# Final norm of a mixture-of-experts layer: nine token tiles beside the last two experts

## The reference, cut to what matters

```python
def rmsnorm(x, g):
    xf = x.astype(jnp.float32)
    y = xf * lax.rsqrt(jnp.mean(xf * xf, axis=-1, keepdims=True) + EPS)
    return (y * g.astype(jnp.float32)).astype(x.dtype)

def ec_moe(h, w_router, w_g, w_u, w_d):
    cap = EC_FACTOR * n // N_EXPERTS
    aff = jax.nn.softmax((h @ w_router).astype(jnp.float32), axis=-1)
    vals, idx = lax.top_k(aff.transpose(0, 2, 1), cap)
    xg = jax.vmap(lambda hb, ib: hb[ib])(h, idx)
    ...
    y = jnp.einsum('becf,efd->becd', jax.nn.silu(a) * u, w_d) * vals[..., None].astype(h.dtype)
    return ...zeros((n, D)).at[ib.reshape(-1)].add(yb.reshape(-1, D))

    x = x + g2 * ec_moe(h2, ...)
    y_prompt, y_sample = rmsnorm(xp, final_norm), rmsnorm(xs, final_norm)
```

## Time and profile before

| | |
|---|---|
| runs shown (3) | 3118.61, 3133.28, 3135.63 us |
| median | 3133.28 us |
| profiled execution | span 3119.0 us from first to last instruction; no time of its own is given beside the span |
| mean granted TensorE clock | 0.965 |
| instructions | 43740 |

### The profile page before, as it was taken

How to read it: one execution, slowest core, us unless ns; L and a number is a source line. 1 busy time by engine, 2 the same in 40 slices (tenths; PEclk the granted TensorE clock), 3 DMA queues, 4 the chain that set the end, 5 groups by cost and what they waited for, 6 DMA issues and landing times. The chain is left out here.

```text
span 3119.0 us, 43740 instructions
## 1 busy us (share of the span) xinstructions
PE 2902.1 (93%) x16786; PEld 2329.5 (75%) x16786; DVE 1992.4 (64%) x2606; ACT 1086.4 (35%) x1720; POOL 1066.2 (34%) x688
## 2 busy tenths in 40 slices
PE   6999999999789999999999999989937999999993
PEld 3888888888667777777777767878826888888882
DVE  5418292829348888878888865555675556566655
ACT  5311111111344444444444443223313333433344
POOL 1000000000123344444333546421106765656652
PEclk8999999999889999999999999999968999999996
DMA  6212232211541110110111146675414666666657
GB/s 231 100 51 106 80 105 80 106 66 55 185 139 24 27 32 13 27 34 16 23 27 33 34 132 191 190 251 165 154 59 156 200 203 200 188 202 206 202 184 285
DMA packets 139523, 371.24 MB, mean 119 GB/s; under 512 B 20886, under 2 KB 47996, under 8 KB 129116
## 3 DMA queue, kind: packets, MB, share of 16 engines
q1 hardware_dynamic: 99820, 266.47, 25.8%
q0 software_dynamic: 23984, 74.71, 8.7%
q10 hardware_dynamic: 15552, 27.79, 2.5%
HBM read 265.99 MB, written 102.89 MB: 118 GB/s over the span
## 5 line engine op out<-in xcount | busy, mean ns | idle before, releaser
L1176 ACT ACTIVATE at_w<-banks 128x512 f32<-128x512 f32 (+1 forms) x592 | 347.6, 591 | 467.1 <-PE banks L1282 410.9
L1398 DVE TENSOR_REDUCE at_mpart<-banks 128x2 f32<-128x512 f32 x584 | 374.1, 683 | 140.2 <-PE banks L1309 140.0
L1254 POOL TENSOR_TENSOR at_part<-at_part,at_w 128x512 f32<-128x512 f32 x224 | 296.8, 1325 | 331.1 <-ACT at_w L1176 327.8
L2598 POOL TENSOR_TENSOR moe_gu_lo<-raw,moe_gu_hi 128x2048 fp32r<-128x2048 f32 x63 | 293.3, 4660 | 110.7 <-ACT moe_gu_hi L2665 110.3
L517 DVE SCALAR_TENSOR_TENSOR fr_r<-fr_r,fr_dw 128x2334 f32<-128x2334 f32 x120 | 318.0, 2650 | 3.9
L374 PE MATMUL fr_po<-hT_hi,fr_w_hi 128*128 128x512 f32 (+1 forms) x800 | 297.0, 371 | 3.0 <-PE fr_po L374 1.8
L374 PE MATMUL fr_po<-hT_lo,fr_w_hi 128*128 128x512 f32 (+1 forms) x800 | 294.7, 368 | 0.0
L374 PE MATMUL fr_po<-hT_hi,fr_w_lo 128*128 128x512 f32 (+1 forms) x800 | 294.7, 368 | 0.0
L1321 PE MATMUL banks<-at_w,V 128*64 128x256 f32 (+1 forms) x2368 | 283.0, 381 | 0.0
L2786 DVE TENSOR_TENSOR moe_d_lo<-moe_raw_d,moe_d_hi 128x1024 fp32r<-128x1024 f32 x64 | 198.1, 3095 | 106.4 <-ACT moe_d_hi L2697 106.4
L1425 DVE TENSOR_TENSOR at_part<-at_part,at_w 128x512 f32<-128x512 f32 x224 | 231.7, 1034 | 13.0
(11 more groups left out here) (415 smaller groups left out, 6805.9 us busy)
## 6 DMA issues: line engine op xcount, KB each, us to landing
raw<-w_gate_up SPq DMA_DIRECT2D x64, 1024.0 KB
moe_raw_d<-w_down SPq DMA_DIRECT2D x64, 512.0 KB, 4.5
fr_wm<-w_ada_rows POOLq DMA_DIRECT2D x32, 512.0 KB, 4.5
gates_scratch<-fr_r ACTq DMA_DIRECT2D x64, 256.0 KB, 2.0
mx_gates<-gates_scratch SPq DMA_DIRECT2D x64, 256.0 KB, 3.1
fr_raw<-w_in SPq DMA_DIRECT2D x28, 512.0 KB, 5.4
fr_r<-x POOLq DMA_DIRECT2D x18, 512.0 KB, 5.6
raw<-mixed_scratch SPq DMA_DIRECT2D x9, 1024.0 KB, 6.2
```

What stands on the lines that cost most here:

```text
L1176: act.activation(w[:, g % NW, k, 0:n], sc[:, (2 * g + k) % SCB, 0:n], ACT.Exp, scale=SM_SCALE).then_inc(exp_done, 1)
L1254: pool.tensor_tensor(part[:, j % 2, 1, 0:n], before, w[:, g % NW, 1, 0:n], ALU.add).then_inc(add_p, 1)
L1398: dve.tensor_reduce(mpart[:, s, 2 * half:2 * half + 2, c], max_bank(m, half), AX.X, ALU.max).then_inc(red_done, 1)
L2598: pool.tensor_tensor(gu_lo[:, slot], raw_gu[:, slot], gu_hi[:, slot].bitcast(F32), ALU.subtract).then_inc(glo_done, 1)
```

## The change

Tiles 0 to 8 are loaded during the last expert: SP issues the norm's weights and tiles 0 to 2 behind the down weights of piece 60 (after waiting for the scatter of expert 13), tiles 3 to 5 behind those of piece 61, tiles 6 to 8 behind those of piece 62; tiles 9 to 17 come as before, after the scatter of expert 14. Tiles 0 to 7 are normed in pairs at the ends of pieces 59, 60, 61 and 62 and stored by POOL one piece later. Tiles 8 to 11 are done in the last piece, at the place where 0 to 3 were. Behind it come three groups of three (12 to 14, 15 to 17, and 18 to 20). Within a group all squares are done first, then all roots, all reciprocals, all scalings.

Numbers 18 to 20 are new: since tiles 0 to 8 are now read before expert 14 adds its part, that expert's rows (two times 128 and 32 of full width) are gathered again after its scatter into weight buffers that are free by then (`old_rows`), normed like tiles, and written over the tiles' rows; only then are the rows of expert 15 written. The scatter of expert 14 now waits for the loads of tiles 0 to 8. Six semaphores are new, and two earlier phases clear a few of theirs at their end (`p.numbers`).

```diff
@@ attention_phase and mix_phase @@
+        p.numbers.append(norm_ld.num)
+        p.numbers += [sem.num for sem in (*c_ld, *o_st, inv_ld)]
@@ moe_phase @@
-    BEFORE, LATE, LATER = 4, 9, 13
+    DONE_IN = {(E - 2, 3): (0, 1), (E - 1, 0): (2, 3), (E - 1, 1): (4, 5), (E - 1, 2): (6, 7), (E - 1, 3): (8, 9, 10, 11)}
+    AFTER = ((12, 13, 14), (15, 16, 17), (18, 19, 20))
+    LOAD_IN = ((0, 1, 2), (3, 4, 5), (6, 7, 8), range(9, TILES))
...
+        old_rows = [raw[:, 0:D], raw[:, D:2 * D], raw_d[0:CAPP, 0]]
+        old_ld, old_st = p.sems("old_ld", 3), p.sems("old_st", 3)
+        def rows_of(n):
+            return fx[:, n % U] if n < TILES else old_rows[n - TILES]
...
@@ SP, in load(), behind the down weights @@
+                        if last:
+                            load_tokens(m)
+                def load_tokens(m):
+                    if m == 0:
+                        load_norm()
+                    if m in (0, M - 1):
+                        for i in range(3):
+                            sp.wait_ge(y_st[i], 16 * (E - 2 if m == 0 else E - 1))
+                    for n in LOAD_IN[m]:
+                        if n >= U:
+                            sp.wait_ge(f_st[n % U], 16 * (n // U))
+                        j = ORDER[n]
+                        sp.dma_start(fx[:, n % U], t["x2"][j * P:(j + 1) * P, :]).then_inc(fx_ld[n % U], 16)
@@ POOL, scatter() @@
+                    if isinstance(e, int) and e == E - 2:
+                        for n in range(U):
+                            pool.wait_ge(fx_ld[n], 16)
@@ POOL, gather_rows(), behind the gathers of expert 15's rows @@
+                    pool.wait_ge(glo_done, M * E - 1)
+                    pool.wait_ge(d_mm, M * E - 3)
+                    for i, (_, n) in enumerate(SL):
+                        pool.indirect_dma_start(old_rows[i], None, t["x2"],
+                                                bass.IndirectOffsetOnAxis(ap=idx_s[0:n, 0, i:i + 1], axis=0)).then_inc(old_ld[i], 16)
+                def store_tokens(ns):
+                    for n in ns:
+                        pool.wait_ge(f_done, n + 1)
+                        j = ORDER[n]
+                        pool.dma_start(t["y"][j * P:(j + 1) * P, :], fx[:, n % U]).then_inc(f_st[n % U], 16)
@@ POOL, expert() and behind it @@
+                        if last and m < M - 1:
+                            store_tokens(done_in(*((e, m - 1) if m else (e - 1, M - 1))))
                         if m == 2 and last:
                             gather_rows()
+                            store_tokens(done_in(e, m))
...
-                pool.wait_ge(out_done, 3)
+                store_tokens(range(8, TILES))
                 for u in range(U):
                     pool.wait_ge(f_st[u], 16 * (TILES // U))
+                pool.wait_ge(f_done, TILES + 3)
+                pool.sem_inc(may_issue, 1)
+                for i, (_, n) in enumerate(SL):
+                    pool.indirect_dma_start(t["y"], bass.IndirectOffsetOnAxis(ap=idx_s[0:n, 0, i:i + 1], axis=0), old_rows[i], None
+                                            ).then_inc(old_st[i], 16)
+                for i in range(3):
+                    pool.wait_ge(old_st[i], 16)
+                pool.wait_ge(out_done, 3)
@@ ACT; DVE has normed(ns) in the same places @@
-                            for n in range(BEFORE):
-                                squares(n)
+                            squares(done_in(e, m))
...
+                        if not (last and m == M - 1):
+                            squares(done_in(e, m))
                 pairs(act, expert)
-                for n in range(BEFORE, LATE):
-                    squares(n)
+                for ns in AFTER:
+                    squares(ns)
                 for i in range(2):
                     act.wait_ge(z_done, i + 1)
...
-                for n in range(LATE, LATER):
-                    squares(n)
                 act.wait_ge(zms_done, 2)
                 act.activation(root_l[:], mean_l[:], ACT.Sqrt).then_inc(zroot_done, 1)
-                for n in range(LATER, TILES):
-                    squares(n)
@@ DVE, normed(ns) @@
+                    for n in ns:
+                        u, c = n % U, rows_of(n).shape[0]
+                        dve.wait_ge(sq_done, n + 1)
+                        wait(dve, root_done, n - U + 1)
+                        dve.tensor_scalar(meansq[0:c, u:u + 1], sumsq[0:c, u:u + 1], 1.0 / D, EPS, ALU.mult, ALU.add).then_inc(ms_done, 1)
+                    for n in ns:
+                        u, c = n % U, rows_of(n).shape[0]
+                        dve.wait_ge(root_done, n + 1)
+                        dve.reciprocal(rstd[0:c, u:u + 1], root[0:c, u:u + 1]).then_inc(rstd_done, 1)
...
+                    for n in ns:
+                        u, x = n % U, rows_of(n)
+                        c = x.shape[0]
+                        dve.wait_ge(rstd_done, n + 1)
+                        dve.scalar_tensor_tensor(out=x, in0=x, scalar=rstd[0:c, u:u + 1], in1=norm[0:c],
+                                                 op0=ALU.mult, op1=ALU.mult).then_inc(f_done, 1)
```

More of the change, by code:

```diff
@@ L2512, in moe_phase, with done_in @@
             p.sem("norm_ld"), p.sems("fx_ld", U), p.sems("f_st", U), p.sems("row_ld", 3), p.sems("row_st", 3))
+        old_ld, old_st = p.sems("old_ld", 3), p.sems("old_st", 3)
+        def rows_of(n):
+            return fx[:, n % U] if n < TILES else old_rows[n - TILES]
+        def done_in(e, m):
+            return DONE_IN.get((e, m), ()) if isinstance(e, int) else ()
         sq_done, ms_done, root_done, rstd_done, f_done = (
@@ L2671, in x_hi_part, with squares @@
                                    turned_in(e, i, half)[:, 0:4 * n].rearrange("p (k n) -> p k n", k=4), ACT.Copy).then_inc(xhi_done, 1)
-                def squares(n):
-                    u = n % U
-                    act.wait_ge(fx_ld[u], 16 * (n // U) + 16)
-                    wait(act, sq_done, n - 1)
-                    wait(act, rstd_done, n - U + 1)
-                    act.activation(fsq[:, n % 2], fx[:, u], ACT.Square, accum_out=sumsq[:, u:u + 1]).then_inc(sq_done, 1)
-                    act.wait_ge(ms_done, n + 1)
-                    act.activation(root[:, u:u + 1], meansq[:, u:u + 1], ACT.Sqrt).then_inc(root_done, 1)
+                def squares(ns):
+                    for n in ns:
+                        u, x = n % U, rows_of(n)
+                        c = x.shape[0]
+                        if n < TILES:
+                            act.wait_ge(fx_ld[u], 16 * (n // U) + 16)
+                        else:
+                            act.wait_ge(old_ld[n - TILES], 16)
+                        wait(act, sq_done, n - 1)
+                        wait(act, rstd_done, n - U + 1)
+                        act.activation(fsq[0:c, n % 2], x, ACT.Square, accum_out=sumsq[0:c, u:u + 1]).then_inc(sq_done, 1)
+                    for n in ns:
+                        u, c = n % U, rows_of(n).shape[0]
+                        act.wait_ge(ms_done, n + 1)
+                        act.activation(root[0:c, u:u + 1], meansq[0:c, u:u + 1], ACT.Sqrt).then_inc(root_done, 1)
                 split_gu(0, 0, 0)
@@ L2757, in scale_y, with normed @@
                                              op0=ALU.mult, op1=ALU.mult).then_inc(y_done, 1)
-                def normed(n):
-                    u = n % U
-                    dve.wait_ge(sq_done, n + 1)
-                    wait(dve, root_done, n - U + 1)
-                    dve.tensor_scalar(meansq[:, u:u + 1], sumsq[:, u:u + 1], 1.0 / D, EPS, ALU.mult, ALU.add).then_inc(ms_done, 1)
-                    dve.wait_ge(root_done, n + 1)
-                    dve.reciprocal(rstd[:, u:u + 1], root[:, u:u + 1]).then_inc(rstd_done, 1)
-                    dve.wait_ge(rstd_done, n + 1)
-                    dve.scalar_tensor_tensor(out=fx[:, u], in0=fx[:, u], scalar=rstd[:, u:u + 1], in1=norm[:],
-                                             op0=ALU.mult, op1=ALU.mult).then_inc(f_done, 1)
+                def normed(ns):
+                    for n in ns:
[3 more added lines that the diff above has]
+                        dve.tensor_scalar(meansq[0:c, u:u + 1], sumsq[0:c, u:u + 1], 1.0 / D, EPS, ALU.mult, ALU.add).then_inc(ms_done, 1)
+                    for n in ns:
+                        u, c = n % U, rows_of(n).shape[0]
+                        dve.wait_ge(root_done, n + 1)
+                        dve.reciprocal(rstd[0:c, u:u + 1], root[0:c, u:u + 1]).then_inc(rstd_done, 1)
+                    if ns == DONE_IN[E - 2, M - 1]:
+                        dve.wait_ge(norm_ld, 16 * 6)
+                    for n in ns:
+                        u, x = n % U, rows_of(n)
+                        c = x.shape[0]
+                        dve.wait_ge(rstd_done, n + 1)
+                        dve.scalar_tensor_tensor(out=x, in0=x, scalar=rstd[0:c, u:u + 1], in1=norm[0:c],
+                                                 op0=ALU.mult, op1=ALU.mult).then_inc(f_done, 1)
```

(10 more changed lines are left out.)

20 lines of the change are left out of this document (6 added, 14 removed).

## The result

Before takes 3131.03 us (median of 20 runs, 3118.61 to 3135.88), the change 3135.65 us (20 runs, 3129.48 to 3141.33). The ratio is 1.0018 [1.0011, 1.0025]: slower by 0.18%, some 5.6 us. That is within the 0.5% named beforehand and inside the range, but the interval is clear of 1, and the sum had said -0.6 us.

A forecast was written before the change was run, and what follows sets the result against it. PE was taken to bound the experts up to 3051, then ACT, DVE and POOL the last 68 us. A loss of 13.5 us less a gain of 14.1 gave -0.6 us, 3132.7 us on the median; range 3115 to 3144.

The forecast's parts named there:

- The loop that is not hidden: Pieces 59 to 63: norm work stands in the loop ACT, DVE, POOL and loses 13.5 us before the tail.
- The wait of 3.7 us forecast before piece 63: End of piece 61: PE, ready at 3055.1, waits 3.7 us for gu_lo(63), then is 7.7 us late.
- The collision: DVE's tile scaling and POOL's subtraction hold each other; bounds: none, or up to 1.2 us on POOL, 4.6 on DVE per piece.
- The tail: From the end of d_hi(63) to POOL's final stores: 40.1 us instead of 54.2, a gain of 14.1 us.
- the ring comes round late: Rival, tail: loads wait for stores of earlier tiles; +2 us by medians, up to +6.4 (3139); chance 0.12.
- point of decision: Ring rival, tile 17's load behind tile 8's store: decides once a store and a load together take over 11.6 us.
- The argument against the rival: Against a late ring in the tail: traffic is now spread, nine loads are over before it.
- Groups save about 3: Tail check: grouping tiles saves about 3 us; a group of three costs 4.5 us against 5.4.
- The end: Final stores to kernel end: 12.5 us as before, from 3105.9 to 3118.4.
- Table switches: Rival: six added switches (nine for three) each hold ACT for twice the load, sum grows 7.7 us to 3140; chance 0.03.
- Hidden after all: Rival, last expert: d_hi(63) late only by its own pair, 3.9 us; total -10.2 us, 3123; chance 0.12.
- The level: Whole kernel: the runs' median is 14.3 us above the profiled execution; the difference is put on the median, giving 3132.7 us.

The follow-up runs named there:

- noin: The change with tiles 0 to 8 still loaded early but none normed in pieces 59 to 62 (0 to 3 in piece 63): 3135.93 us, ratio 1.0020.
- spare: The change with tiles 15, 16 and 17 loaded into free weight buffers, so their loads wait for no store: 3132.21 us, ratio 0.9999.
- late: The change with the gathers of expert 14's rows issued behind the stores of tiles 8 to 11: 3129.55 us, ratio 0.9994.
- sparelate: The change with tiles 15 to 17 in free weight buffers and expert 14's gathers behind the stores of tiles 8 to 11: 3132.11 us, ratio 1.0000.
- group: The kernel before with its tiles in groups, all squares of a group first, then roots, reciprocals, scalings: 3133.8 us, ratio 1.0013.
- best2: The change with twelve buffers, one pair at piece 59, tiles 2 to 5 singly in piece 63, old rows gathered behind tile 5's store: 3129.32 us, ratio 0.9998.
- copyroot: The change with the Sqrt of the tiles replaced by a Copy, which needs no table load: 3134.04 us, ratio 1.0008.
- best3: As best2, but expert 14's rows gathered where the change has them, ahead of the stores: 3130.09 us, ratio 1.0004.
- alt12: As noin12, but tiles 0 and 1 normed at the end of piece 59, 2 and 3 at the end of 61: 3131.66 us, ratio 0.9994.
- best: As best2, but expert 14's rows gathered behind the store of tile 11: 3131.82 us, ratio 1.0004.
- noin12: As noin, with a ring of twelve buffers in place of nine: 3132.1 us, ratio 0.9988.

## Why the prediction was right or wrong

**The sign of the sum was wrong; the size is 5.5 us off.** By its own terms, each taken from the x_hi copy:

- *The loop that is not hidden, +13.5.* Measured +11.34: right in mechanism, 2.2 too much. The piece at 61 fits to a few tenths (gu_hi forecast to end at 3026.5, measured 3026.3 after the shift of 7.13), and `noin` shows that nothing else costs here. What was too much is no single step: ACT's copies end 0.2, 0.7, 1.5 and 2.2 us ahead of the forecast from pair to pair (gu_hi of 61, 62 and 63, then d_hi). POOL's subtraction starts beside DVE's scaling and is stretched by 0.5 to 0.65, and so ends only 0.1 to 0.2 us before a full wait for the scaling would let it; the rest is steps that I rounded up. gu_lo(62) starts at 3039.1 where I put 3040.6, gu_lo(63) at 3051.9 in place of 3054.2. PE is late by 0.5, 3.1 and 6.1 us, forecast 0.8, 4.0 and 7.7. The wait of 3.7 us forecast before piece 63 did not come as a wait: piece 62 ran 2.9 us longer in its place (last section).
- *The collision.* Taken like d_lo, and rightly: 5.26, 5.12 and 5.21 us for POOL's subtraction, 5.44 for d_lo. The Trainium skill's rule that a DVE instruction with two SBUF inputs contends with a GpSimd one that reads SBUF (SBUF — State Buffer, Who interferes with whom) agrees with these rows. The copy of indices, held for 4.50 us, has only one input.
- *The tail, -14.1.* Measured -7.06. This is the step that failed. I gave 40.1 us from the end of d_hi(63) to the final stores; it took 47.2 (48.22 from its start). The work was sized well: less ACT's waits for loads it is 39.2 in the change, 39.6 in spare, 39.0 in late and 39.6 in sparelate. But I costed the loads of the ring as in time and gave "the ring comes round late" 0.12. The loss is where this rival had it: the group of tiles 15 to 17 took 11.8 us in place of 4.5. Its point of decision (11.6 us for a store and a load) was right, its price (+2 to +6.4) a little low: 7.95 us of waits, 19.35 for the store and the load.
- *Why it was mis-sized.* I took landings of 6.0 and 7.8 us from the earlier trace rows, medians of a tail in which a tile is scaled every 1.8 us. The change makes that faster, puts six gathers beside the stores, and the same engines that were 102% busy in the earlier trace rows answer with 10.7 and 8.0. The argument against the rival, that nine loads are over before the tail, counts bytes that were moved ahead, but the stores and gathers of the tail were packed into fewer microseconds (that is my reading; no run carries fewer bytes). `late` shows what the gathers cost, `spare` what the lack of buffers does: 3.7 us each alone, 4.1 together.
- *Groups save about 3.* `group` says +2.6 on the kernel before, 0.9 of it a wait for a load. It did not spoil the 40.1, which was summed step by step with all squares of a group ahead of its scalings; the 3 stood only in the check beside it.
- *The end, 0.* Measured +0.59, in all kernels derived from the change (12.99 to 13.07 us) and not in group (12.41). Its cause was not tried.
- *Table switches.* Nine loads, as forecast, of 1.28 us each, and the next step 0.02 behind one. The Trainium skill's drain of 1.38 us beside each (ScalarE: Activation LUTs, What ACT_TABLE_LOAD costs) is not to be seen: taking away the seven loads up to d_hi(63), four of them on ACT's way, gave 2.2 us, less than 4 x 1.28 (in one of the four places POOL's scatter bound instead).
- *Hidden after all.* Fell: d_hi(63) was 11.34 us late, not 3.9. But a single pair is nearly hidden (0.53 in best2), so this rival holds for the first pair alone.
- *The level.* I put the difference on the median and not on the profiled execution. This was right, though without a reason at the time: the trace of before had an early front. That the forecast of 3132.7 is only 3 us from the measured 3135.65 is in part luck, for before itself moved from 3133.28 in the three runs shown to 3131.03 in 20. What the runs showed against the text's 0.5% is that 20 executions of each tell 0.07% of this kernel, and 7 to 12 tell 0.09 to 0.15%.

## What to carry to other kernels

Work moved beside a busy engine is free only up to the slack of the loop that feeds this engine, and the first portion costs little where the next cost more: price each portion by itself. When a phase bound by a full DMA loses compute work, ask first how long a store and a reload take at the new pace, since the landing times in the old trace are those of the old pace. For effects of a few microseconds in milliseconds, compare the stretch that was changed, starting at an instruction that was not changed.

## What was not expected of the hardware

A short wait of PE was followed by half its clock. Stages of the changed kernel about the wait before piece 62 (columns as above):

```profile
3048.00:3051.00 3.00, 0.86 (x10) 0.16 (x8) 3.00 (x1) 0.84 (x2) 3.00 (x1) 0.96 0.00 0
3051.00:3054.00 3.00, 2.56 (x10) 2.56 (x11) 2.40 (x5) 0.99 (x2) 2.83 (x2) 0.50 0.03 5
3054.00:3057.00 3.00, 3.00 (x14) 3.00 (x14) 0.31 (x2) 2.97 (x7) 2.39 (x3) 0.50 0.84 101
3057.00:3060.00 3.00, 3.00 (x23) 3.00 (x21) 2.78 (x5) 2.98 (x5) 3.00 (x4) 0.90 1.05 203
```

PE stood still for 2.58 us, and then worked for some 6 us at a granted clock of 0.50, that is at 1.2 GHz of its 2.4: 14 matmuls in 3 us where the next row has 23. Piece 62 took 12.8 us (3051.44 to 3064.28) in place of the 9.9 of the earlier trace rows. I had counted PE's wait alone and not what follows it. Here it cost nothing, since gu_lo(63) was ready only at 3064.22, but where PE is the bound, a wait of 2.6 us would cost more than twice its length (an estimate: 2.6 and the 2.9 us by which the piece was longer). It does not follow every wait: in copyroot PE waited 1.84 us before piece 62 and the row 3057 to 3059 has 0.50, but behind 1.58 us before piece 63 the row 3068 to 3071 has 1.00.

The other surprise is how far the unchanged front moves: 14 us over 14 executions, 0.45% of the time. It goes with the mean granted clock. The two earliest fronts (before and best3) have the highest, 0.965 and 0.966; the three with 0.960 or 0.961 are at 3032.75 to 3034.79, though two at 0.963 (alt12 and best) are as late. Before's own 35 executions beside noin12 say the same: the nine at 0.960 or less took 3132.62 to 3139.76 us, the six at 0.965 or more 3124.86 to 3129.38. What sets the granted clock of an execution was not tried.
